# Eight recurrence heads: score blocks of two chunks and two carried states a direction, in place of single chunks and four states

## What is computed

```
def hgrn2_chunk_scan(q, k, v, logf, s0):
    """S_t = diag(f_t) S_{t-1} + k_t v_t^T, o_t = S_t^T q_t, in chunkwise form. CHUNK = 64"""
    b = cumsum(logf)                      # inside each chunk
    qe, ke = q * exp(b - b_ref), k * exp(b_ref - b)
    scores = where(tril, qe @ ke^T, 0)
    o_intra = scores @ v
    kv = (k * exp(b_last - b))^T @ v
    s_final, s_start = scan(lambda s, (decay, u): decay * s + u, s0, (exp(b_last), kv))
    o = o_intra + (q * exp(b)) @ s_start
```

## Time and profile before

| | |
|---|---|
| median of 3 runs | 985.67 us (982.87 to 986.67) |
| span of the profiled execution, first to last instruction | 981.3 us |
| TensorE (PE) busy | 946.5 us, 96% of the span |
| weight loads (PEld) busy | 875.5 us, 89% |
| VectorE (DVE) busy | 656.0 us, 67% |
| ScalarE (ACT) busy | 510.0 us, 52% |
| mean granted TensorE clock | 0.990 |
| chain that ended last | PE 91%, DVE 3%, POOL 2%, ACT 1%, DMA 1% |

### The profile page before, as it was taken

One profiled execution on the slowest core, in us unless ns is written; L12 is line 12 of the kernel. 1 busy time (PEld: TensorE's weight loads), 2 busy tenths in 40 slices (PEclk: granted clock), 3 DMA queues, 4 the chain that ended last, 5 costly groups with the idle time before them and its releaser, 6 DMA issues.

```text
span 981.3 us, 18439 instructions
## 1 busy us (share of the span) xinstructions
PE 946.5 (96%) x7012; PEld 875.5 (89%) x7012; DVE 656.0 (67%) x1010; ACT 510.0 (52%) x792; POOL 30.7 (3%) x26
## 2 busy tenths in 40 slices
PE   6799999999999999999999999999999899999995
PEld 2468888888889999999999899999999799999995
DVE  3978477777777577776677866765377575555554
ACT  6543455546664365555555655544464464444442
POOL 0720000000000000000000000000000100000001
PEclk9899999999999999999999999999999999999998
DMA  8579633322332545555555343344454255555441
GB/s 295 181 258 354 233 131 129 129 96 81 122 128 90 169 130 193 190 177 177 181 176 172 132 163 129 135 145 156 151 188 169 73 187 178 191 175 190 173 148 43
DMA packets 45152, 159.92 MB, mean 163 GB/s; under 512 B 5168, under 2 KB 6576, under 8 KB 44976
## 3 DMA queue, kind: packets, MB, share of 16 engines
q1 hardware_dynamic: 43632, 156.56, 46.4%
q10 hardware_dynamic: 1472, 2.69, 0.7%
HBM read 158.18 MB, written 1.05 MB: 162 GB/s over the span
## 4 chain that ended last, share of the span: by engine, by line
PE 91%; DVE 3%; POOL 2%; ACT 1%; DMA 1%; issue 0%; SPq 0%; DVEq 0%; ACTq 0%
PE bank L371 25%; PE bank L373 24%; PE bank L372 24%; PE bank L1047 4%; PE bank L1106 2%; PE bank L1142 1%; PE bank L1108 1%; PE bank L1126 1%; POOL tok L1407 1%; PE bank L1120 1%; PE bank L438 1%; DMA tok<-in_tok 1%; PE bank L1137 1%; PE bank L1061 1%; PE bank L1093 1%; PE bank L1080 1%
## 5 line engine op out<-in xcount | busy, mean ns | idle before, releaser
L365 DVE TENSOR_TENSOR w_lo<-raw,w_hi 128x1024 fp32r<-128x1024 f32 x260 | 317.1, 1232 | 156.8 <-ACT w_hi L358 156.3
L371 PE MATMUL bank<-h_hi,w_hi 128*128 128x256 f32 (+1 forms) x1328 | 396.2, 298 | 2.3 <-DVE h_lo L546 1.0
L373 PE MATMUL bank<-h_hi,w_lo 128*128 128x256 f32 (+1 forms) x1328 | 390.3, 294 | 0.0
L372 PE MATMUL bank<-h_lo,w_hi 128*128 128x256 f32 (+1 forms) x1328 | 389.0, 293 | 0.0
L358 ACT ACTIVATE w_hi<-raw 128x1024 fp32r<-128x1024 f32 x260 | 270.3, 1052 | 116.7 <-PE bank L373 87.0
L371 PEld LDWEIGHTS bank<-h_hi,w_hi 128*128 128x128 f32 x1328 | 251.3, 189 | 12.0 <-issue 4.3
L372 PEld LDWEIGHTS bank<-h_lo,w_hi 128*128 128x128 f32 x1328 | 251.1, 189 | 5.5
L373 PEld LDWEIGHTS bank<-h_hi,w_lo 128*128 128x128 f32 x1328 | 249.7, 188 | 5.7
L371 PE MATMUL bank<-y_hi,w_hi 128*128 128x256 f32 x560 | 158.7, 283 | 0.0
L373 PE MATMUL bank<-y_hi,w_lo 128*128 128x256 f32 x560 | 158.3, 283 | 0.0
L372 PE MATMUL bank<-y_lo,w_hi 128*128 128x256 f32 x560 | 157.4, 281 | 0.0
(11 more groups left out here) (209 smaller groups left out, 994.0 us busy)
## 6 DMA issues: line engine op xcount, KB each, us to landing
raw<-in_stream SPq DMA_DIRECT2D x260, 512.0 KB, 3.3
arena<-in_ada SPq DMA_DIRECT2D x24, 512.0 KB, 5.4
xres<-in_ada SPq DMA_DIRECT2D x8, 512.0 KB, 3.2
tok<-in_tok SPq DMA_DIRECT2D x4, 512.0 KB, 10.0
con<-in_con ACTq DMA_DIRECT2D x1, 1472.0 KB, 10.6
xres<-in_tok ACTq DMA_DIRECT2D x1, 1024.0 KB, 8.6
out<-xres SPq DMA_DIRECT2D x4, 256.0 KB, 2.4
par<-in_par SPq DMA_DIRECT2D x1, 156.5 KB, 10.8
```

What stands on the lines that cost most here:

```text
L365: dve.tensor_tensor(w_lo[c.slot][:, :], raw[c.slot][:, :], w_hi[c.slot][:, :].bitcast(F32), ALU.subtract).then_inc(S("split_lo"), 1)
L371: pe.matmul(dst, hi_w, a_hi, start=start, stop=False, skip_group_check=True)
L372: pe.matmul(dst, hi_w, a_lo, start=False, stop=False, skip_group_check=True)
L373: return pe.matmul(dst, lo_w, a_hi, start=False, stop=stop, skip_group_check=True)
```

## The change

The recurrence is worked in blocks of two chunks (128 tokens). A state is carried from block to block only: two states a direction, and one latent `key_values` product a direction. Scores are 128x128 blocks: the diagonal chunks come from two products that accumulate, of key arrays in which the other half of each chunk is zero (`k_e[0]`: first half, against all 128 queries; `k_e[1]`: second half, against the later half of each chunk); the corner, first chunk's keys against second chunk's queries, is a third product. The queries get a third slot of 64 that holds the second chunk decayed over the first, and the keys of the first chunk are decayed over the second before they are turned. The outputs move from bank 5 to bank 7. Cut to what is spoken of:

```diff
         def kv_at(d, s):
-            c = s - 1 if d == 0 else NCH - s
-            col = 0 if s == 0 else {(0, 1): 1, (0, 3): 2, (1, 2): 3, (0, 2): 1, (1, 1): 2, (1, 3): 3}[d, s]
-            return psum[6 + (d if s == 0 else c % 2)][:, col * P:(col + 1) * P]
+            return psum[6][:, (2 * s + d) * P:(2 * s + d + 1) * P]
+        def block_at(d, s):
+            return s if d == 0 else NB - 1 - s
+        def chunk_of(d, b, late):
+            return 2 * b + (late if d == 0 else 1 - late)
+        def q_slots(p, d):
+            x = q_d[p][:, d * NB * Q_SLOT:(d + 1) * NB * Q_SLOT]
+            return x.rearrange("p (b s c) -> p b s c", b=NB, s=3)
+        def halves(x, late, per=T):
...
+        o_bank = psum[7][:, 0:T]
...
-            def turn(p, part_, bank):
-                for d in range(2):
-                    for b in range(2):
-                        at = d * TC + part_ * T + b * P
+            def turn_latent(bank):
+                for d in range(2):
+                    at = d * TC + block_at(d, 0) * P
+                    last = pe.transpose(psum[bank][:, d * P:(d + 1) * P], k_d[:, at:at + P], ident)
+                last.then_inc(S("k_turned"), 1)
+            def turn_context(bank):
+                for d in range(2):
+                    for b in range(NB):
+                        at = d * TC + T + b * P
                         last = pe.transpose(psum[bank][:, (2 * d + b) * P:(2 * d + b + 1) * P], k_d[:, at:at + P], ident)
...
             def chunk_scores(p):
                 for d in range(2):
-                    behind, ahead = (HALF, 0) if d == 0 else (0, HALF)
-                    for c in range(NCH):
...
+                    for b in range(NB):
+                        x = d * T + b * P
+                        pe.matmul(psum[5][:, x:x + P], k_e[0][:, x:x + P], q_e[:, x:x + P], start=True, stop=False,
+                                  skip_group_check=True)
+                        pe.matmul(late_halves(psum[5], d, b), k_e[1][:, x:x + P], late_halves(q_e, d, b), start=False,
+                                  stop=True, skip_group_check=True)
+                for d in range(2):
+                    for b in range(NB):
+                        first, second = chunk_of(d, b, 0), chunk_of(d, b, 1)
+                        row = CH * (first % 2)
+                        y = d * T + second * CH
+                        k = d * TC + first * CH
+                        near = k_near[:, d * CH:(d + 1) * CH] if b == block_at(d, 0) else k_d[:, k:k + CH]
+                        last = pe.matmul(psum[5][row:row + CH, y:y + CH], near, q_slots(p, d)[:, b, 1, :],
                                          start=True, stop=True, skip_group_check=True)
...
-                    for s in range(1, NCH):
...
+                for d in range(2):
+                    b = block_at(d, 0)
+                    last = pe.matmul(kv_at(d, 1), k_dT[:, d * P:(d + 1) * P], v_cur[:, b * P:(b + 1) * P],
+                                     start=True, stop=True, skip_group_check=True)
                 last.then_inc(S("kv"), 1)
             def outputs(h, p):
-                pe.wait_ge(S("masked"), h * 2 + 2)
-                pe.wait_ge(S("state"), h * 8 + 8)
+                pe.wait_ge(S("masked"), h + 1)
+                pe.wait_ge(S("state"), h * 4 + 4)
...
+                    for d in range(2):
+                        s = block_at(d, b)
+                        last = pe.matmul(dst, state[:, (2 * d + s) * P:(2 * d + s + 1) * P], q_slots(p, d)[:, b, ::2, :],
+                                         start=False, stop=d == 1, skip_group_check=True)
...
-                    pe.wait_ge(S("k_d"), h)
-                    turn(1 - u, 0, 3)
-                    turn(1 - u, 1, 4)
+                    pe.wait_ge(S("k_far"), h * 2)
+                    turn_latent(3)
+                    turn_context(4)
+                    chunk_scores(1 - u)
                     if prev2:
                         pe.wait_ge(S("o_n"), h - 1)
-                    chunk_scores(1 - u)
                     pe.wait_ge(S("qg"), h)
...
             dve.memset(sc_T, 0.0)
+            dve.memset(k_e[0], 0.0)
...
-            dve.memset(psum[5][:, 0:T], 0.0).then_inc(S("scores_cleared"), 1)
+            dve.memset(k_e[1], 0.0)
...
-                dve.tensor_tensor(split2(k_e), split2(e_ke), split2(k_buf)[:, :, 0:T], ALU.mult)
+                for late in range(2):
+                    dve.tensor_tensor(halves(k_e[late], late), halves(e_ke, late), halves(k_buf, late, TC), ALU.mult)
                 dve.wait_ge(S("e_kd"), h + 1)
                 dve.tensor_tensor(k_d, e_kd, k_buf, ALU.mult).then_inc(S("k_d"), 1)
+                for d in range(2):
+                    dve.tensor_tensor(k_near[:, d * CH:(d + 1) * CH], first_chunks(e_kd)[d], first_chunks(k_buf)[d], ALU.mult)
+                dve.wait_ge(S("k_d"), h + 1)
+                for d in range(2):
+                    end = last_token(d, chunk_of(d, block_at(d, 0), 1))
+                    x = first_chunks(k_d)[d]
+                    dve.tensor_scalar(x, x, e_qd[:, end:end + 1], None, ALU.mult).then_inc(S("k_far"), 1)
+                for d in range(2):
+                    ends = split2(e_qd[:, d * T:(d + 1) * T])[:, :, last_token(d, chunk_of(d, 0, 0)) - d * T:][:, :, 0:1]
+                    x = q_slots(p, d)
+                    dve.tensor_tensor(x[:, :, 2 - 2 * d, :], x[:, :, 1, :], ends.broadcast_to([P, NB, CH]), ALU.mult)
+                for d in range(2):
+                    first, second = (last_token(d, chunk_of(d, block_at(d, 0), late)) for late in range(2))
+                    dve.tensor_tensor(e_pair[:, d:d + 1], e_qd[:, first:first + 1], e_qd[:, second:second + 1], ALU.mult)
...
-                for odd in range(2):
-                    rows = slice(CH * odd, CH * odd + CH)
-                    dst = sc_T.rearrange("p (n q t) -> p n q t", q=2, t=CH)[rows, :, odd, :]
-                    dve.copy_predicated(dst, by_tile(msk[rows, :], 4), by_tile(psum[5][rows, 0:T], 4)).then_inc(S("masked"), 1)
+                mask = msk[:, :].rearrange("p (d o c) -> p d o c", d=2, o=1).broadcast_to([P, 2, NB, P])
+                dve.copy_predicated(sc_T.rearrange("p (d b c) -> p d b c", d=2, b=NB), mask,
+                                    psum[5][:, :].rearrange("p (d b c) -> p d b c", d=2, b=NB)).then_inc(S("masked"), 1)
...
-                for s in range(NCH):
...
+                for d in range(2):
+                    dve.tensor_copy(state[:, 2 * d * P:(2 * d + 1) * P], kv_at(d, 0)).then_inc(S("state"), 1)
+                for d in range(2):
+                    dve.wait_ge(S("state"), h * 4 + (d + 1))
+                    dve.scalar_tensor_tensor(state[:, (2 * d + 1) * P:(2 * d + 2) * P], state[:, 2 * d * P:(2 * d + 1) * P],
+                                             e_pair[:, d:d + 1], kv_at(d, 1), ALU.mult, ALU.add).then_inc(S("state"), 1)
```

More of the change, by code:

```diff
@@ L44 @@
 NCH = T // CH
+NB = T // P
+Q_SLOT = 3 * CH
+Q_DIR = NB * Q_SLOT + CH
 D_FF = 2816
@@ L108, in constants @@
     c[:, CON["dist"]:] = np.concatenate([own, prev, own], axis=1)
[L109 to L113, removed]
+    j, i = np.arange(P)[:, None], np.arange(P)[None, :]
+    m = np.stack([j <= i, j >= i], axis=1).astype(np.int32)
+    return c, m.reshape(P, 2 * P)
 OWN_TILES = (0, 1, 4)
@@ L203, in build @@
         con = sb("con", N_CON)
-        msk = sb("msk", 4 * CH, I32)
+        msk = sb("msk", 2 * P, I32)
         par = sb("par", N_PAR)
@@ L262, in build @@
         v_mean = tiny(8)
+        e_pair = tiny(2)
         rstd = part(TC)
@@ L269, in build @@
         q_e = part(2 * T)
-        q_d = [part(2 * T) for _ in range(2)]
-        k_e = part(2 * T)
+        q_d = [part(2 * Q_DIR) for _ in range(2)]
+        k_near = part(2 * CH)
         k_d = part(2 * TC)
         qg = [part(2 * T) for _ in range(2)]
-        k_dT = part(8 * P)
-        state = part(8 * P)
-        sc_T = part(8 * CH)
+        k_e = [part(2 * T), wide[:, 3584:4096]]
+        sc_T = part(2 * NB * P)
+        k_dT = part((2 + 2 * NB) * P)
+        state = part(4 * P)
         v_cur = part(4 * P)
@@ L333, in kv_at, with last_token, q_raw, first_chunks @@
         def kv_at(d, s):
-            c = s - 1 if d == 0 else NCH - s
-            col = 0 if s == 0 else {(0, 1): 1, (0, 3): 2, (1, 2): 3, (0, 2): 1, (1, 1): 2, (1, 3): 3}[d, s]
-            return psum[6 + (d if s == 0 else c % 2)][:, col * P:(col + 1) * P]
+            return psum[6][:, (2 * s + d) * P:(2 * s + d + 1) * P]
[3 more added lines that the diff above has]
+            return 2 * b + (late if d == 0 else 1 - late)
+        def last_token(d, c):
+            return d * T + c * CH + (CH - 1 if d == 0 else 0)
+        def q_slots(p, d):
+            x = q_d[p][:, d * NB * Q_SLOT:(d + 1) * NB * Q_SLOT]
+            return x.rearrange("p (b s c) -> p b s c", b=NB, s=3)
+        def q_raw(p):
+            x = q_d[p].rearrange("p (d r) -> p d r", d=2)[:, :, 0:NB * Q_SLOT]
```

(33 more changed lines are left out.)

44 lines of the change are left out of this document (10 added, 34 removed).

## The result

The changed kernel takes 952.5 us in the median of four runs (951.26 to 954.58), the kernel before 984.66 (982.87 to 986.67): the ratio is 0.967, 95% interval 0.965 to 0.969. I had forecast 963.5 us with a range of 957.5 to 970.0. The direction and the bound were right; the gain was 32 us and not 22, outside the range. (The kernel before has a fourth run here, which moved its median from 985.67 to 984.66.)

What follows compares the result with a forecast made beforehand. TensorE was taken to bound each head, before and after. From the 985.67 us median, 20.8 us for shorter TensorE blocks in 8 heads and 1.4 for the clock were taken off, giving 963.5 us, range 957.5 to 970.

Steps and rivals of the forecast that it cites:

- the ten added operations: VectorE, around the decayed keys and queries: small added products and a split one, +1.74 us a head in all.
- the mask: VectorE: goes from two operations of 64 partitions x 256 (0.92 us) to one of 128 x 512, taken as 0.9.
- Rival B: VectorE becomes the bound at 25.8 us a head if added operations cost 0.68 each; 976 us, chance 0.04.
- rival C: TensorE works strided operands as two pieces each, 1.7 us a head more; 977 us, chance 0.03.
- Rival D: TensorE stands waiting for `k_far`, a head 1.0 us longer; slower at 994 us, chance 0.02.
- full records: TensorE products with 128 weight columns: 0.11 us each in key-values and outputs; 0.12 for each turn transpose.
- entry costs: TensorE, key-values: 0.09 us extra that the first four records took on entry, added to 1.32 to give 1.41.
- exit of 0.20: TensorE, end of the corner group in the scores: 0.20 us added for the change of shape, bounds 0 and 0.40.
- corner term: TensorE scores: eight corner records at 0.105 us, 0.84 a head, plus 0.20 for the change of shape.
- Rival A: TensorE scores: alternating shapes were the cost, so corners take 0.42 us, not 0.84; 958.5 us, chance 0.10.
- low clock in one head: Granted clock fell to 0.52 behind one score block; its 1.4 us, once in eight heads, was forecast as saved.

Runs made afterwards that it cites:

- fourfold key product: The changed kernel with the 1024-column product of the decayed keys done four times, each behind the one before; 972.01 us in one run.
- combined kernel: The changed kernel with diagonal scores done by the old narrow products without zero padding, all score products grouped by width; 945.52 us against 983.55 for the kernel before.
- split outputs: The changed kernel with each output product of a state and 128 query columns split into two of 64 columns; 965.11 us in one run.
- grouped kernel: The kernel before with its 16 score products a head issued in two groups, eight of 64 key columns, then eight of 32; 959.92 us against 984.18.

## Why the prediction was wrong where it was

**Right: the bound.** TensorE sets the length of a head before and after, VectorE stays behind it, and no wait took the place of what was removed. VectorE ended at 19.65 us a head instead of 20.8: the ten added operations cost 1.2 us and not 1.74 (L1637 to L1649 take 1.14 from start to start), and the mask (L1677, 246.93 to 247.56) 0.63 instead of 0.9. That is 0.8 of the 1.15 us; the rest was not taken apart. Rival B had no ground, and in rival C the strided operands are worked in one piece: L1188 has four records a block and not eight. Rival D needed a delay that only the fourfold key product made.

**Right in kind, a little high: full records.** 12 key-value, 16 output and 6 transpose records cost 0.105 to 0.11 and no entry; with 0.11 to 0.12 and entry costs I was 0.31 us a head too high, 2.5 us in all.

**Wrong: the step from the rows to a price for small records.** I wrote that all small records lie between 0.085 and 0.12 whatever their shape, and that "it is their number that counts". The low and the high end of that came from L1106 and L1108, which alternate between 64 and 32 weight columns. Most of their price was that of the change of width, about 0.175 us each time, and not of the record. Inside a group of one width a 64-column record costs 0.03 (0.034 in the corners, 0.031 in the combined kernel) and a 32-column one 0.026, or 0.011 where neighbours write different rows. The exit of 0.20 in the sum was about right, since the change back to 128 columns took 0.15. What was mis-sized is the record: the seven steps between the eight corner records took 0.24 us where the sum has 0.84 for the eight. So the corner term was 0.39 us and not 1.04; 0.65 of the miss, of which the full score records, 1.83 us and not 1.72, took 0.11 back. With the 0.31 of the full records the miss is 0.85 us a head, 6.8 us in all.

Rival A was this mechanism, at 0.42 us for the corners, and I gave it 0.10. That 0.42 lies near the measured 0.39 by luck: it has 0.05 a record and no exit, where the runs show 0.03 and an exit of 0.15. What I held against A was no argument: L1142, all of one shape, is not cheaper than L1106's pair because its weights have 128 columns, as the split outputs show again. The rows that should have weighed more are the second L1120 group with its 0.20 us and the odd fact that a record of L1106, smaller than L1137's in both operands, was dearer, 0.12 against 0.11. The Trainium skill (TensorEngine Tiling (Array Packing), Tiling Modes) says that a change of the tiling mode drains TensorE. The runs agree in that a change of shape costs time, about 0.175 us here in fp32 for a change of width and 0.20 for one of weight rows; what that time is spent on they don't show. The Trainium skill (TensorE: Matmul & The Clock Gate, LDWEIGHTS) puts a weight load at its columns divided by 1.2 in ns, that is an estimated 0.107, 0.053 and 0.027 us for 128, 64 and 32 columns. The measured 0.105 and 0.026 a record lie close to it at 128 and at 32 columns; at 64 the measured 0.03 is little more than half of the estimate. Why 64 columns are so cheap was not tested.

**The remaining 3 us.** The heads gave 27.6 and the low clock in one head 1.4 in the profiled executions; the medians differ by 32.2. The changed kernel's profiled execution was its slowest, 954.58 us, 2.1 above the median. That of the kernel before was a quick one: in its other runs the time is 1.8 us above the span, so a span of 981.3 goes with an estimated 983.1, 1.5 below the median. Together this is the remaining 3 us, within half a us. The changed kernel's profile has a stretch of lower clock before the heads (0.57 from 51.5 to 55.5 us), and its mean granted clock was 0.990 where its other three runs have 0.993; whether that made it the slowest was not tested. Nor was why single executions differ by such amounts before the heads, as in the run with split outputs.

**The clock.** The mean granted clock was 0.984 to 0.990 in the 21 runs of the kernel before that were made beside the experiments, and 0.992 to 0.994 in the four of the grouped kernel. The profile of the grouped kernel shows no stretch at the lower level inside the heads, as that of the changed kernel shows none. That fits a lower clock behind the alternating scores, but it was not tested by itself. Part of the difference in the mean lies outside the heads, in the stretch from 777.1 us that the grouped profile lacks, and the corner products between the full ones alternate widths too, with a mean of 0.993.

## What to carry to other kernels

On a TensorE that never idles, put neighbouring small products in groups of the same weight width before redesigning them: here the mere order gained 24 us, the redesign 32 (19 of them by fewer full records in the turn, the key-values and the outputs, 8.5 in the scores), and the two together 38. Take the price of a small matmul from a group of its own shape and add the change at both ends, never from a stretch in which shapes alternate; where a smaller shape is not the cheaper one, suspect the neighbours. Padding narrow products to full blocks to save their number buys less than grouping them does.

## What the hardware showed that I had not expected

A change of weight width between two fp32 products cost 0.173 to 0.177 us (14 fewer changes saved 2.42 us a head in the old scores, some of it by overlap; 6 more cost 1.06 in the new). Inside a group of one width the price of a record did not follow its weight columns: 0.105 to 0.11 us at 128, 0.03 at 64 and 0.026 at 32 on the same rows, so that going from 64 to 32 saved almost nothing. Products of 32 weight columns overlapped when they wrote different 32-row groups, 0.011 us a record, while 64-column products that alternate between two 64-row halves gained nothing by it (0.38 us against 0.39). And 64 moved columns against 128 weight columns cost as much as 128.
